# Attention inside a fused two-model kernel: the steps alternate between the two heads of a pair

## The reference

```python
def dilated_attention_mixer(h, w_qkv, q_gain, k_gain, w_o, rel_bias):
    qkv = (h @ w_qkv).reshape(b, s, N_ATTN_GROUPS, 3, HEADS_PER_GROUP, HEAD_DIM)
    for g, (window, dil) in enumerate(((128, 1), (512, 4), (2048, 16))):
        q = head_rms_norm(qkv[:, :, g, 0], q_gain[g])
        k = head_rms_norm(qkv[:, :, g, 1], k_gain[g])
        v = qkv[:, :, g, 2]
        o, l = dilated_group_attention(q, k, v, bias_g, dil, (window // 2) // dil)
        ...
    wts = jax.nn.softmax(jnp.stack(lses, axis=0), axis=0)
    o = jnp.einsum('gbsh,gbshe->bshe', wts, jnp.stack(outs, axis=0))
    return o.reshape(b, s, ATTN_OUT) @ w_o
```

## Time and profile before

| | |
|---|---|
| median of 3 runs | 2628.02 us (2627.02 to 2633.07) |
| the profiled execution: time / span of the trace | 2635.66 us / 2633.9 us |
| PE busy, PEld busy | 93%, 89% of the span |
| DVE, ACT, POOL busy | 60%, 45%, 26% |
| mean granted TensorE clock | 0.952 of full speed |
| attention's stages 2 to 6, each | 32.9 us |

### The profile page before, as it was taken

How to read it: one execution, slowest core, us unless ns; L and a number is a source line. 1 busy time by engine, 2 the same in 40 slices (tenths; PEclk the granted TensorE clock), 3 DMA queues, 4 the chain that set the end, 5 groups by cost and what they waited for, 6 DMA issues and landing times. The chain is left out here.

```text
span 2633.9 us, 54753 instructions
## 1 busy us (share of the span) xinstructions
PE 2448.5 (93%) x22034; PEld 2347.2 (89%) x22034; DVE 1590.5 (60%) x2781; ACT 1191.2 (45%) x1921; POOL 678.6 (26%) x440
## 2 busy tenths in 40 slices
PE   8999798999999998999999997889997999979998
PEld 7999688999889998899999987789997888869998
DVE  3779696666524555566566679736667455335665
ACT  3543464444444554444344455444444344523443
POOL 1230396000185443100000056530003454510000
PEclk9999699999999999999999998999997999859999
DMA  4565100455455442355345543225542222203552
GB/s 168 185 197 187 63 1 18 161 186 180 132 184 151 117 117 87 124 185 182 106 155 180 194 143 120 97 96 192 191 136 75 82 83 74 81 10 128 185 183 95
DMA packets 103293, 344.47 MB, mean 131 GB/s; under 512 B 16336, under 2 KB 22000, under 8 KB 102592
## 3 DMA queue, kind: packets, MB, share of 16 engines
q1 hardware_dynamic: 102560, 340.66, 39.9%
q0 software_dynamic: 544, 1.12, 0.3%
HBM read 340.56 MB, written 1.16 MB: 130 GB/s over the span
## 5 line engine op out<-in xcount | busy, mean ns | idle before, releaser
L151 PE MATMUL ps<-h_high,hi 128*128 128x256 f32 x3320 | 972.8, 293 | 47.9 <-DVE h_low L294 26.0
L153 PE MATMUL ps<-h_high,lo 128*128 128x256 f32 x3320 | 952.3, 287 | 2.0 <-issue 2.0
L152 PE MATMUL ps<-h_low,hi 128*128 128x256 f32 x3320 | 952.9, 287 | 0.0
L101 ACT ACTIVATE hi<-raw 128x1024 fp32r<-128x1024 f32 x623 | 644.2, 1051 | 379.1 <-PE ps L153 378.6
L123 POOL TENSOR_TENSOR lo<-raw,hi 128x1024 fp32r<-128x1024 f32 x183 | 437.9, 2401 | 1331.3 <-ACT hi L101 1331.1
L151 PEld LDWEIGHTS ps<-h_high,hi 128*128 128x128 f32 x3320 | 650.5, 196 | 63.7 <-DVE h_low L294 29.1
L123 DVE TENSOR_TENSOR lo<-raw,hi 128x1024 fp32r<-128x1024 f32 x440 | 530.2, 1225 | 216.4 <-ACT hi L101 215.8
L152 PEld LDWEIGHTS ps<-h_low,hi 128*128 128x128 f32 x3320 | 650.6, 196 | 0.7
L153 PEld LDWEIGHTS ps<-h_high,lo 128*128 128x128 f32 x3320 | 650.4, 196 | 0.0
L151 PE MATMUL ps<-hidden_high,hi 128*128 128x256 f32 x1056 | 296.7, 281 | 8.1 <-DVE lo L123 7.7
L152 PE MATMUL ps<-hidden_low,hi 128*128 128x256 f32 x1056 | 298.8, 283 | 0.0
(11 more groups left out here) (448 smaller groups left out, 3641.4 us busy)
## 6 DMA issues: line engine op xcount, KB each, us to landing
raw<-in_weights SPq DMA_DIRECT2D x623, 512.0 KB, 3.6
at_bias<-bias_group SPq DMA_DIRECT2D x64, 64.0 KB, 2.7
s_bn<-in_s_bn SPq DMA_DIRECT2D x4, 512.0 KB, 4.5
consts<-in_consts SPq DMA_DIRECT2D x1, 1506.5 KB, 8.6
x<-in_x SPq DMA_DIRECT2D x1, 1024.0 KB, 4.8
s_cT<-in_s_b SPq DMA_DIRECT2D x1, 1024.0 KB, 7.8
s_cw<-in_s_c SPq DMA_DIRECT2D x1, 1024.0 KB, 10.0
s_cT<-s_rows POOLq DMA_DIRECT2D x16, 64.0 KB, 7.3
```

The source lines that it names most:

```text
L101: act.activation(k.hi[:, item % CUT, :], k.raw[:, item % RAW, :], ACT.Copy).then_inc(k.item_rounded, 1)
L151: pe.matmul(out, wh, xh, start=start, stop=False, **more)
L152: pe.matmul(out, wh, xl, start=False, stop=False, **more)
L153: return pe.matmul(out, wl, xh, start=False, stop=stop, **more)
```

## The change

The four steps of a pair are ordered half by half, so that steps `q` and `q + 1` (`q` even) are the two heads of the pair for the same query positions. `scores(q)` and `values(q)` now each do both heads, and their matmuls alternate between the halves of the array: one matmul for head 0, one for head 1, and so on. They are called for even `q` only. `transposed` stays one step at a time, and ACT and DVE keep their order; only which head and which half a step number stands for changes there.

```diff
-        steps = [(h, b) for h in range(AH) for b in range(2)]
+        steps = [(2 * n + hh, b) for n in range(HP) for b in range(2) for hh in range(2)]
...
             def scores(q):
-                h, b = steps[q]
-                p0, n = 64 * (h % 2), h // 2
+
+                n, b = q // 4, steps[q][1]
                 pe.wait_ge(a.kn, n + 1)
                 if q >= 2:
-                    pe.wait_ge(a.max, q - 1)
+                    pe.wait_ge(a.max, q)
                 for g in range(GROUPS):
                     keys = slice(0, T) if g == 0 else slice(b * P, (b + 1) * P)
                     col = 0 if g == 0 else T + (g - 1) * P
-                    mm = pe.matmul(k.ps[:, S0 + q % 2, col:col + (T if g == 0 else P)], qT[p0:p0 + 64, n % 2, g, b * P:(b + 1) * P],
-                                   kT[p0:p0 + 64, n % 2, g, keys], start=True, stop=True, tile_position=(p0, 0))
-                mm.then_inc(a.sc, 1)
+                    for hh in range(2):
+                        rows = slice(64 * hh, 64 * hh + 64)
+                        mm = pe.matmul(k.ps[:, S0 + hh, col:col + (T if g == 0 else P)], qT[rows, n % 2, g, b * P:(b + 1) * P],
+                                       kT[rows, n % 2, g, keys], start=True, stop=True, tile_position=(64 * hh, 0))
+                        if g == GROUPS - 1:
+                            mm.then_inc(a.sc, 1)
...
             def values(q):
-                h, b = steps[q]
-                p0, n = 64 * (h % 2), h // 2
-                pe.wait_ge(a.cp, q + 1)
+
+                n, b = q // 4, steps[q][1]
+                pe.wait_ge(a.cp, q + 2)
...
                 for j in range(4):
-                    mm = pe.matmul(k.ps[p0:p0 + 64, PV, b * P:(b + 1) * P], vs[j][:, h * 64:(h + 1) * 64],
-                                   pt[:, q % 2, j * P:(j + 1) * P], start=(j == 0), stop=(j == 3), tile_position=(0, p0))
-                mm.then_inc(a.pv, 1)
+                    for hh in range(2):
+                        h = 2 * n + hh
+                        mm = pe.matmul(k.ps[64 * hh:64 * hh + 64, PV, b * P:(b + 1) * P], vs[j][:, h * 64:(h + 1) * 64],
+                                       pt[:, hh, j * P:(j + 1) * P], start=(j == 0), stop=(j == 3), tile_position=(0, 64 * hh))
+                        if j == 3:
+                            mm.then_inc(a.pv, 1)
...
                     transposed(q - 2)
-                    values(q - 3)
-                    scores(q - 1)
+                    values(q - 4)
                 beside(s, 1)
-                if s > 1:
-                    values(q - 2)
...
                 if s > 1:
-                    values(q - 1)
+                    values(q - 2)
...
                 transposed(q)
-                scores(q + 1)
                 if s < HP:
                     sums(PER * s + 3)
                 beside(s, 5)
-                values(q)
                 transposed(q + 1)
                 scores(q + 2)
```

## The result

The changed kernel takes 2596.42 us (median of 4 runs, 2594.99 to 2598.89); the kernel before, run beside it, 2630.55 (2627.02 to 2634.38). The ratio is 0.9857, with a 95% interval of 0.9838 to 0.9876: 1.4% faster, 34.1 us by the medians. In a second session, on another chip, the changed kernel took 2599.63 and the kernel before 2633.7, ratio 0.9872 (0.9851 to 0.9894). Forecast were 2598.3 and a gain of 29.7.

What follows compares the result with a forecast made beforehand. PE was taken to bound attention. Gains of 2.2 (stage 1), 20.2 (six full stages), 5.3 (stage 8) and 2.0 (tail) sum to 29.7, so 2628.0 - 29.7 = 2598.3 us; range 2591 to 2614.

Steps and rivals of the forecast that it cites:

- Side by side, both kinds: In attention's scores and values, two heads on different halves of PE overlap; likeliest case, 2598.3 us, chance 0.77.
- The rival that alternations cost 0.05 us or more: In pairs of scores and values, each change of half empties the array; at 0.1 us each 2637 us, chance 0.05.
- Nothing side by side: In scores and values no heads overlap, only changes of division are saved: gain 10 us, 2618 us, chance 0.07.
- Scores in series: Only values overlap; scores in series cost 13.9 us, 2612 us; chance 0.08 for one kind only.
- The excess of a pair: A pair of scores or values on PE was taken to cost 0.1 us over a single block.
- The wait before the first `sums`: In stages 2 to 7, PE waits 0.72 us for ACT's square before the stage's first sums.
- The transposes in the middle: PE's mid-stage transposes were called close to having to wait, some 0.1 us.
- A full stage: Each of stages 2 to 7: 4.48 out, 0.4 excess and 0.72 wait back, 3.36 less, about 29.6 us.
- Stage 8: Last norm starts earlier, 3.3 us; blocks removed after the idle, 2.3 less 0.3; together 5.3 us, idle about 3.9.
- if the clock stays up: Stage 8's 24 products after the idle would gain 2.3 us more at the upper clock; not in the sum.
- The first stage and the tail: Stage 1 and the tail behind stage 8, one scores and one values block less each: 2.2 and 2.0 us.
- The scale: The 29.7 us sum, from the profiled execution of 2635.66 us, was subtracted from the runs' median of 2628.0.

Runs made afterwards that it cites:

- only_values_alternate: Changed kernel with a pair's scores in series (head 0, then head 1) while values still alternate; 2601.19 us, ratio 0.9872.
- square_and_diagonal_first: Changed kernel with ACT's first square of a stage right behind the roots and DVE's diagonal ahead of the two key instructions; 2590.57 us, ratio 0.9859.

## Why the prediction was right, step by step

**Side by side, both kinds: right, and shown.** The two kernels that exchange loops and the one that puts a pair into one half give the three levels 1.02, 1.51 and 1.89 us for values, 1.08, 1.61 and 1.95 for scores. The rival that alternations cost 0.05 us or more is out: at 7 alternations the whole pair is within 0.01 us of one head. "Nothing side by side" was priced at 2618, and the kernel that is just that took 2617.01; but the price was a gain of 10 and attention gave 15.3. The full stages gave 8.5 (6 forecast), stage 8 4.5 (3.7), the first stage and the tail 0.8 and 1.4 (0.5 each, less 0.8 for a later signal that did not show). That the times agree is luck: the kernel before ran at 2632.46 beside it, where the price was laid on 2628.0. "Scores in series" was priced with nothing given back; by `only_values_alternate` half of it is given back at the wait for ACT's square (0.77 to 0.29 us).

**The excess of a pair: mis-sized.** The prediction took 0.1 us over a single block, from caution about the clock; the timeline shows 0.01. That is 32 pairs by 0.1, 3.2 us, of which the waits take some back.

**The wait before the first `sums`: right.** Counted by starts, as the prediction did, it is 0.77 us (5.74 less 4.97), where 0.72 was forecast. The `sums` behind the wait takes 0.47 us to the next product, as it did in the earlier trace rows behind values (866.64 to 867.11), so this changes nothing in the sum. The profile's 0.61 is less because it counts from the end of the last product and not from the next start.

**The transposes in the middle: right, with a cause unseen.** They were called close, and they wait 0.09 us: in the earlier trace rows they came 3.42 us after the `sums` ahead of them, in the changed kernel 3.51. What the prediction missed is the instruction held by POOL. The diagonal was not held in the kernel before (0.29 us), so its rows could not show this; the one hint was the last key tile, 2.66 us in the earlier trace rows and 0.67 in the earlier trace rows. The question left out is what POOL does beside DVE once DVE's work moves.

**A full stage.** 4.48 out, 0.04 of excess, 0.77 and 0.09 of waits: 3.58. Measured are 3.66 (21.94 by six), and 3.36 was forecast. The 0.08 that is left was not traced.

**Stage 8: right in kind, 1.6 us short.** The norm starts when ACT's roots are there. DVE's timeline in the changed kernel:

```profile
998.40 0.23 DVE L1688 RECIPROCAL at_q_inverse<-at_q_root 128x12 f32<-128x12 f32 x1 [2.40 <-ACT at_q_root L1565]
...
1003.05 0.29 DVE L1720 TENSOR_SCALAR at_diag<-consts,at_stats 128x128 f32<-128x128 f32 x1
...
1005.03 0.67 DVE L1681 SCALAR_TENSOR_TENSOR at_k<-at_k_raw,at_gain,at_root 128x256 f32<-128x256 f32 x1
```

The idle time is 3.85 us, and 3.9 was forecast. The products behind it take 4.44 us (1005.80 to 1010.24) where they took 5.25: the clock comes back to its upper level during them, and 0.8 of the 2.3 us that the prediction priced apart "if the clock stays up" came. The stretch right behind is shorter too, 7.76 us against 8.21, at a mean clock of 1.00 against 0.94; the two executions of the kernel without the waits, 7.77 at 1.00 and 8.14 at 0.95, put 0.4 of that on the clock. So some 1.2 of the 33.7 us are the clock's, which is not shown to be the change's. The three excesses of 0.1 priced here did not show either.

**The first stage and the tail** gave 2.6 and 2.3 for 2.2 and 2.0; two and one pairs without excess are about half of it, and the rest was not traced.

**The scale.** The sum was set against the profiled execution and then laid on the medians. That was the right choice: some 4.7 us of that execution were the clock in the S5 layer, which the medians don't have. Luck has a part in how near the time came: the gain was forecast 4.4 us too small, but the kernel before ran at 2630.55 beside the changed one and not at the 2628.02 of the forecast, so the time is only 1.9 us off.

**The rule on weight loads.** The Trainium skill, "TensorE: Matmul & The Clock Gate", section "The mechanism", has weight loads overlap matmuls in flight only when the row group differs. For the values all 128 rows are in use in both halves, and 16 records go through in 1.03 us against 1.89 in one half. The measurement differs from the rule, and decides.

## What to carry to other kernels

When two small matmuls use different halves of PE, by rows or by columns, write them in turns, one by one; in series only half of the overlap comes, and within one half none. Put them into common blocks too: here the merging alone gave 15 of 34 us, by the prediction's reasoning through fewer changes between ways of dividing the array and scores that come earlier for the engines behind (no experiment tells the two apart). Then read the next two waits of PE together: removing the first gave nothing, because PE already met the second, by 0.1 us. And when a change moves one engine's work in time, look at what the others do at its new place: here DVE's diagonal slid under POOL's subtraction.

## What the runs showed of the hardware

PE begins with records of the other half although three earlier ones of the first half have not started: 0.49 us after the first head's start, of the 0.87 that its eight records take, for column halves, and 0.54 for row halves. With the values in turns by twos it is three again, and there the second head starts after 0.01 us.

A DVE instruction can be held for as long as POOL works: 1.73 us in place of 0.29 for the diagonal (`consts` by a scalar, all in SBUF), 2.67 in place of 0.67 for a key tile with `at_k_raw` and `at_root` in SBUF. The ends lie 0.08 and 0.49 us after the end of POOL's instruction. The same key line with its second operand in PSUM kept its 1.07 for two in `square_and_diagonal_first`, though POOL worked from 854.88 on. The Trainium skill, "SBUF — State Buffer", section "Who interferes with whom", says that a VectorE instruction with two SBUF inputs, or in a two-port mode, and a GpSimd one that reads SBUF shut each other out for a whole instruction, and that with one SBUF input otherwise there is no contention; these rows agree, as to which instructions are stretched and by how much; that the diagonal, with one input tensor, runs in a two-port mode is not shown by any row.
